# Bias store moved behind the last weight split; routing with halved searches, merged top-k lists, host-turned p and an early gather

## The reference, cut to what matters

```
h = RMSNorm(x); qA,kA,vA,qB,kB,vB = h @ W_in
A: windowed attention (|q-k| <= 128), sink logit per head,
   bias rel_bias[t5_bucket(k-q)] shared by all tokens, 8 heads
B: dense attention with normalised q/k and axial rotary positions, 8 heads
x += concat(RMSNorm_A(oA), RMSNorm_B(oB)) @ W_out
h = RMSNorm(x); aff = softmax(h @ W_router)              # 16 experts
per set (sample, prompt): gates, idx = top_k(aff.T, cap) # cap 128 of 1024, 64 of 512
x += scatter_add(idx, gates * (silu(h[idx] @ Wg) * (h[idx] @ Wu)) @ Wd)
x += sigmoid(RMSNorm(x) @ W_pg) * (p @ W_pp)             # p: 256 wide
y = RMSNorm(x)
```

## Time and profile before

| | us |
|---|---|
| three runs | 1563.09, 1562.75, 1559.45 (median 1562.75) |
| profiled execution | 1559.1 (span 1557.1) |
| PE busy | 1429.2 (92%) |
| DVE busy | 919.7 (59%) |
| ACT busy | 725.8 (47%) |
| POOL busy | 183.3 (12%) |
| mean granted TensorE clock | 0.957 |

### The profile page before, as it was taken

How to read it: one execution, slowest core, us unless ns; L and a number is a source line. 1 busy time by engine, 2 the same in 40 slices (tenths; PEclk the granted TensorE clock), 3 DMA queues, 4 the chain that set the end, 5 groups by cost and what they waited for, 6 DMA issues and landing times. The chain is left out here.

```text
span 1557.1 us, 21333 instructions
## 1 busy us (share of the span) xinstructions
PE 1429.2 (92%) x7224; PEld 1006.1 (65%) x7224; DVE 919.7 (59%) x1324; ACT 725.8 (47%) x1157; POOL 183.3 (12%) x257
## 2 busy tenths in 40 slices
PE   7979997999999798699999699999999999959997
PEld 6758886656555555478877566666666666628885
DVE  4624443777776588432367847766676676653544
ACT  4534444777766577322223444445444444432332
POOL 1111110000000000000001201211121121021110
PEclk9989997999999889799998899999999999979999
DMA  7464465211222133444433747787788778672331
GB/s 297 117 156 160 148 212 200 77 68 66 85 96 99 52 134 126 158 147 137 162 108 127 273 172 252 253 268 256 257 275 274 254 252 262 237 243 75 128 135 68
DMA packets 83709, 267.28 MB, mean 172 GB/s; under 512 B 7968, under 2 KB 37792, under 8 KB 68296
## 3 DMA queue, kind: packets, MB, share of 16 engines
q1 hardware_dynamic: 75456, 239.32, 42.5%
q0 software_dynamic: 7168, 25.17, 7.0%
q10 hardware_dynamic: 1032, 2.10, 1.2%
HBM read 199.98 MB, written 66.58 MB: 171 GB/s over the span
## 5 line engine op out<-in xcount | busy, mean ns | idle before, releaser
L1875 DVE TENSOR_TENSOR moe_w_lo<-ring,moe_w_hi 128x2048 fp32r<-128x2048 f32 x96 | 220.3, 2296 | 157.4 <-ACT moe_w_hi L1814 157.4
L1814 ACT ACTIVATE moe_w_hi<-ring 128x2048 fp32r<-128x2048 f32 x96 | 183.6, 1914 | 201.2 <-PE moe_p_g L1997 122.8
L1525 PE MATMUL mix_p_big<-kept_out_w,mix_m_hi 128*128 128x512 f32 x384 | 126.9, 412 | 4.6 <-DVE mix_m_lo L1400 2.4
L550 PE MATMUL proj_p_out<-proj_w_hi,proj_h_hi 128*128 128x512 f32 x288 | 118.5, 411 | 10.4 <-DVE proj_w_lo L461 10.3
L2005 PE MATMUL moe_p_gu<-ring,moe_xT_r 128*64 128x512 f32 x512 | 116.9, 598 | 0.0
L550 PE MATMUL proj_p_out<-proj_w_hi,proj_h_lo 128*128 128x512 f32 x288 | 113.9, 395 | 0.0
L550 PE MATMUL proj_p_out<-proj_w_lo,proj_h_hi 128*128 128x512 f32 x288 | 113.7, 395 | 0.0
L1073 DVE TENSOR_REDUCE sample_ntop<-sample_p_s 128x1 f32<-128x1024 f32 x64 | 78.1, 1222 | 41.7 <-PE sample_p_s L896 40.9
L910 PEld LDWEIGHTS sample_p_t<-kept_ident_r,sample_probs_r 128*128 128x128 f32 x688 | 72.7, 141 | 23.7 <-ACT sample_probs L1011 6.5
L1525 PEld LDWEIGHTS mix_p_big<-kept_out_w,mix_m_hi 128*128 128x128 f32 x384 | 73.0, 195 | 21.5 <-issue 2.7
L910 PE MATMUL sample_p_t<-kept_ident_r,sample_probs_r 128*128 128x128 f32 x688 | 80.0, 246 | 4.9 <-ACT sample_probs L1011 2.4
(11 more groups left out here) (292 smaller groups left out, 3059.6 us busy)
## 6 DMA issues: line engine op xcount, KB each, us to landing
ring<-in_w_gate SPq DMA_DIRECT2D x32, 1024.0 KB, 5.1
ring<-in_w_up SPq DMA_DIRECT2D x32, 1024.0 KB, 7.0
ring<-in_w_down SPq DMA_DIRECT2D x32, 1024.0 KB, 5.7
qT_d<-proj_qT SPq DMA_DIRECT2D x12, 1024.0 KB, 3.8
proj_xT<-in_xT SPq DMA_DIRECT2D x12, 512.0 KB, 3.9
proj_w_raw<-in_w_in SPq DMA_DIRECT2D x8, 768.0 KB, 6.6
proj_x<-in_x SPq DMA_DIRECT2D x12, 512.0 KB, 5.7
kT_d<-proj_kT SPq DMA_DIRECT2D x12, 512.0 KB, 3.5
```

The lines of the kernel that those rows point to most:

```text
L550: mm = pe.matmul(p_out[:, s, cols], h[:, s, k, :], w[:, k, cols], start=(k == 0 and n == 0), stop=(k == KC - 1 and n == 2))
L1525: mm = pe.matmul(p_out[:, cols], m[:, s, k, :], ww[:, k, cols], start=(k == 0 and n == 0), stop=(k == KC - 1 and n == 2))
L1814: act.activation(w_hi[:, at % SPLIT], raw[:, at % RAW], ACT.Copy).then_inc(hi_made, 1)
L1875: dve.tensor_tensor(w_lo[:, at % SPLIT], raw[:, at % RAW], w_hi[:, at % SPLIT].bitcast(F32), ALU.subtract).then_inc(lo_made, 1)
```

## The change

**Bias rows.** They are loaded between weight chunks 2 and 3. PE looks them up after chunk 3 of `first_products`, DVE adds before `low_w(5)`, ScalarE stores right behind `high_w(7)`, before the squares of tiles 0 and 1.

```diff
@@ project_inputs
+            bias.load(sp, rel_bias, hot, outside)      # SP, after load_w(2)
             load_w(3)
...
                 high_w(k)
+            bias.store(act, rel_d)
             square(0, 0)
...
+                if k == 5:
+                    bias.add(dve)
                 low_w(k)
...
+                    if k == 3:
+                        bias.look_up(pe)
...
-                if isinstance(t, int) and t == 1 and begin == 0:
+                if first and begin == 0:
                     pe.wait_ge(bias.added, 1)
...
             product(2, 0, 0, spread(0))
-            bias.look_up(pe, qk_copied, 6)
```

```diff
@@ mix_and_route
+        SEARCHES = ((0, EXPERTS, S_HALF, CAP), (32, EXPERTS, S_HALF, CAP), (64, 32 + EXPERTS, P_HALF, HALF))
+        ROUNDS = [size // 8 for _, _, _, size in SEARCHES]
+        OPS = [3 * n - 1 for n in ROUNDS]
...
+            def step(t, s, takes):
+                searches = 1 if t < SAMPLE_TILES + 2 else 2
                 if inside(t):
                     low(t, s)
                 if inside(t - 3):
-                    copy_aff(t - 3, 1 - s)
-                search(first, last)
+                    copy_aff(t - 3)
+                searching.take(takes[0], searches)
                 if inside(t - 1):
                     add_x(t - 1, 1 - s)
                 if inside(t - 2):
                     top(t - 2)
+                searching.take(takes[1], searches)
                 if inside(t - 1):
                     norm(t - 1, 1 - s)
                 if inside(t - 2):
                     affinity(t - 2)
+                searching.take(takes[2], searches)
...
+            for t in range(1, N):
+                step(t, t % 2, (6, 2, 6) if t >= SAMPLE_TILES // 2 + 2 else (0, 0, 0))
+            copy_aff(N - 3)
+            searching.take(6)
+            add_x(N - 1, 1)
+            top(N - 2)
+            searching.take(1)
+            affinity(N - 2)
+            norm(N - 1, 1)
+            copy_aff(N - 2)
+            searching.take(8)
             top(N - 1)
+            searching.take(1)
             affinity(N - 1)
-            copy_aff(N - 1, 1)
...
+            searching.take(sum(OPS))
+            list_sample()
+            copy_aff(N - 1)
+            search(2, 0, 6)
+            merge(0, 0, S_HALF, 0)
+            search(2, 6, OPS[2])
+            list_prompt()
+            merge(1, PROMPT_ROW, P_HALF, T_SAMPLE)
```

**p.** The host gives p transposed; one load brings all of it. ScalarE rounds it (`split_p`, one operation), POOL makes the low part, both now with four buffers (AHEAD = 4) instead of two, as has the product `ple`. `product_p(0)` goes to the PSUM area of the turned input and no longer waits for `add_x`; `product_p(1)` waits for it. PE's order at the end:

```diff
             turn_m(0, 0)
             run(pe, step, N)
-            turn_p(0, 0)
-            turn_p(1, 1)
             step(N, 0)
...
+            product_p(0)
+            product_p(1)
             turn_aff(N - 2)
             turn_h(N - 1, 1)
...
+            product_p(2)
             logits(N - 1)
...
+            product_p(3)
             turn_aff(N - 1)
...
+            product_p(4)
+            turn_lists(0)
+            for t in range(5, 8):
+                product_p(t)
+            turn_lists(1)
+            for t in range(8, N):
+                product_p(t)
```

**Gather.** POOL gathers expert 0's rows in the routing stage, behind its last `low_p`:

```diff
+            for t in range(AHEAD, N):
+                low_p(t)
+            for s in range(2):
+                pool.wait_ge(h_stored[s], 8 * N)
+            pool.wait_ge(mm_done, 2 * N)
+            pool.wait_ge(handed, 2)
+            expert_rows.gather_sample(pool, 0)
+            pool.wait_ge(handed, 4)
+            expert_rows.gather_prompt(pool, 0)
```

In `experts` the split of the first turned rows goes ahead of the second weight unit's on ACT and DVE, the first `gate_up` waits for two of the three parts, and PE turns the prompt rows of expert 0 behind its first unit instead of ahead of it:

```diff
             split(0, 0)
+            x_high(0)                                  # DVE: x_low(0)
             split(0, 1)
-            x_high(0)
...
-                    pe.wait_ge(t_out, x_round(e) + X_ROUNDS)
+                    pe.wait_ge(t_out, x_round(e) + X_ROUNDS - 1)
...
+                    if is_int(e) and e == 0 and j == 0:
+                        turn_x_prompt(0)
```

More of the change, by code:

```diff
@@ L1378, in _ @@
                 w_p.high(act, k)
[L1379 to L1388, removed]
+            for t in range(1, 4):
+                step(t, t % 2)
+            for t in range(AHEAD):
+                split_p(t)
             with act.Fori(2, N // 2) as i:
                 for k in range(2):
[L1391 to L1394, removed]
+                    step(i * 2 + k, k)
+            step(N, 0)
+            out_p(0)
+            copy_hT(N - 1)
+            out_p(1)
+            softmax(N - 1)
+            for t in range(2, N):
+                out_p(t)
         @block.vector
@@ L1427, in affinity, with copy_aff @@
                 dve.tensor_scalar(aff[:], e_r[:], share[:], None, ALU.mult).then_inc(aff_made, 1)
[L1429 removed]
+            def copy_aff(t):
                 dve.wait_ge(affT_made, t + 1)
[L1431 to L1436 removed]
@@ L1438, in search @@
-            def search(first, last):
+                if t < SAMPLE_TILES:
+                    row, c = 32 * (t // 4), t % 4 * P
+                else:
+                    row, c = 32 * (2 + (t - SAMPLE_TILES) // 2), t % 2 * P
+                dve.tensor_copy(work[row:row + EXPERTS, 0, c:c + P], p_aff).then_inc(affT_out, 1)
+            def search(which, first, last):
+                row, n_rows, tokens, _ = SEARCHES[which]
+                rows = slice(row, row + n_rows)
+                rounds_ago, strikes_ago = sum(ROUNDS[:which]), sum(n - 1 for n in ROUNDS[:which])
@@ L1458, in search, with backwards, list_sample @@
                         dve.match_replace(there, best[rows, eight], here, -1.0).then_inc(struck, 1)
-            def step(t, s, first=0, last=0):
+            def backwards(ap):
+                step, n = ap.ap[1]
+                return bass.AP(ap.tensor, ap.offset + (n - 1) * step, [ap.ap[0], [-step, n]])
+            def list_sample():
+                dve.wait_ge(indexed, sum(ROUNDS[:2]))
+                one, two = slice(0, EXPERTS), slice(32, 32 + EXPERTS)
+                dve.tensor_copy(place[one, :], at[one, :]).then_inc(listed, 1)
+                dve.tensor_copy(value[one, :], best[one, :]).then_inc(listed, 1)
+                dve.tensor_copy(place[two, :], backwards(at[two, :])).then_inc(listed, 1)
+                dve.tensor_copy(value[two, :], backwards(best[two, :])).then_inc(listed, 1)
@@ new lines, in list_prompt @@
+            def list_prompt():
+                dve.wait_ge(indexed, sum(ROUNDS))
+                for row, order in ((64, lambda ap: ap), (96, backwards)):
+                    rows = slice(row, row + EXPERTS)
+                    for out, ap in ((place, at), (value, best)):
+                        dve.tensor_copy(out[rows, :].rearrange("p (a c) -> p a c", a=2),
+                                        order(ap[rows, 0:HALF]).unsqueeze(1).broadcast_to([EXPERTS, 2, HALF])).then_inc(
+                                            listed, 1)
@@ new lines, in _, with __init__, take @@
+            class Searching:
+                def __init__(self):
+                    self.which, self.done = 0, 0
+                def take(self, n, searches=2):
+                    while n and self.which < searches:
+                        part = min(n, OPS[self.which] - self.done)
+                        search(self.which, self.done, self.done + part)
+                        self.done, n = self.done + part, n - part
+                        if self.done == OPS[self.which]:
+                            self.which, self.done = self.which + 1, 0
@@ L1744, in _ @@
             step(E)
-            for s in range(2):
-                sp.wait_ge(ple_stored[s], 8 * TILES)
+            for done in ple_stored:
+                sp.wait_ge(done, 16 * TILES // len(ple_stored))
             for m in range(PG_UNITS):
@@ L1777, in scatter @@
                         compute_op=ALU.add).then_inc(added, 16)
-            for e in range(3):
+            for e in range(1, 3):
                 gather(e)
```

236 lines of the change are left out of this document (115 added, 121 removed).

## The result

The changed kernel takes 1553.33 us (median of 9 runs, 1548.97 to 1556.5), the kernel before on the same chip 1559.91 us (9 runs, 1556.94 to 1564.61). The ratio is 0.9947, with a 95% interval of 0.9932 to 0.9962: 6 to 11 us faster, where 26 were forecast. 1553.33 lies just above the range's upper end of 1553. The profiled execution took 1551.5 us with a span of 1549.5, so its span is 7.6 us shorter than before's 1557.1.

A forecast was written before the change was run, and what follows sets the result against it. TensorE, busy 92% of the span, was taken as the bound, so only its losses could be won. Bias part 12 plus routing part 14 made 26 us: 1533 for the profiled execution, 1537 on the median's scale, range 1525 to 1553.

The forecast's parts named there:

- Bias part, removed: Projection: moving the bias store removes TensorE's 11.2 us idle at 80 us and 2.1 us of clock, 13.5 us at most.
- The cover for lookup and add: Projection: lookup after chunk 3 and add before split 5 cost nothing; if the cover failed, 3 us.
- Bias part, added: Projection: tile 0's qT_d store, behind the moved bias store, lands in 12.5 us, 1.5 us late; bias part nets +12.
- rival 3: Projection: the bias store does to tile 0 what it did to tile 1, 26.9 us; 1553 us in all; chance 12%.
- Search operations: Routing, VectorE: a top-8 operation shrinks with its width, from 1.25 us to 0.72 at 512 and 0.45 at 256.
- rival 2: Routing: narrow top-8 operations cost as much as wide ones; 1606 us, slower; chance 7%.
- Steps and the first ple product: Routing loop: six steps lengthen by 0.4 us each, yet the first ple product starts at 828.4, 7.9 us earlier.
- Rival 1: Routing: the clock falls in the six lengthened steps, some 2.2 us a place; gain 15, 1548 us; chance 20%.
- Ple products: Routing: twelve products of 2.73 us; TensorE stands 4.3 us for the prompt lists and ends at 869.
- End of the stage: Routing: after ScalarE's copy and SP's store and weight load, the stage ends about 870.5 against 880.16, 9.7 us earlier.
- Experts' start: Experts: 11.5 us from slots to first expert matmul become 5.9; the prompt rows' turn between the first units costs 0.6.
- The sum: Whole kernel: bias part 12 plus routing part 14 gives 26 us, 1533 for the profiled execution.

The follow-up runs named there:

- run 3: Changed kernel with the bias rows held twice, stored from 16 partitions instead of 8, 64 rows each: 1536.85 us, ratio 0.9836 to the kernel before.
- run 1: Kernel before with the bias part of the change alone: 1561.46 us, ratio 1.0001 to the kernel before.
- run 2: Changed kernel with the bias part undone, so the routing part alone: 1553.43 us, ratio 0.9942 to the kernel before.
- run 8: Changed kernel with bias store on 16 partitions, prompt lists turned behind ple product 9, first prompt gather issued in the experts stage: 1528.93 us, ratio 0.9791.
- Run 6: Changed kernel with TensorE's turn of the prompt lists behind ple product 9 instead of 7: 1548.68 us, ratio 0.9917 to the kernel before.
- run 7: Changed kernel with bias store on 16 partitions and prompt lists turned behind ple product 9: 1532.44 us, ratio 0.9813 to the kernel before.

## Why the prediction was wrong

**Bias part, removed: right.** The stall was worth about the 13.5 us that the prediction gave it: run 3, which has it nowhere, ends the projection 13.2 us before the changed kernel and 14.2 before the kernel before. The cover for lookup and add held: no new wait of TensorE stands near 25 us.

**Bias part, added: the step that failed.** "At 49.6 the bias store is 23 us old, not 8, and its early backlog has been worked off: I take 12.5 us". There is no early backlog that is worked off. The store is quick only in its first 3 us (34 rows a us), then moves 24 a us until 64 us and 13 in the last 10 us, which it shares with SP's queue. It lasts from 28 to 74 us, and at 50 us it was as much in the way as ever. qT_d landed after 21.2 us: 10.8 us of stand and some 3 of clock (0.50 from 70.9 to 78.2 us) instead of 1.5. The range of the term was right (-4 to +13.5) and run 1 put it at 0; the value was taken at the wrong end, against the only row with a store of qT_d inside a bias store. My rival 3 was the mechanism, at 12%.

I had also dismissed that row's meaning. I took the q's store as "eight rows an engine" that would each wait for one bias row. The trace of the changed kernel fits longer turns: nothing on q1 in 57 to 63 us, while each of the 8 busy engines passed 144/8 = 18 bias rows, and nothing in 39 to 50 us, 264/8 = 33 rows, with a store open on q1 both times. The Trainium skill ("DMA: Bandwidth & Descriptors", Queues, rings and completion order) says an engine changes queues only after a whole packet, which is several descriptors long; I had read a packet as one row. The trace agrees that an engine stays for many rows; but where the page gives 9 to 17 descriptors as typical and 64 as the most, 33 rows and more passed here before SP's queue had its turn. Why the store uses 8 engines is told by the same page (Why a DMA increments its semaphore by 16 and not by 1): the number of engines is the largest up to 16 that divides the outermost dimension of both sides, here 8 heads. Run 3 agrees, with 16: q10's share went from 47% to 76% and, in 34 to 40 us, 83%.

**Search operations: right,** 0.72 and 0.46 us; rival 2 is out. MAX8 at 512 takes 674 to 685 ns in all 32 instances, FIND_INDEX8 672 to 686 and MATCH_REPLACE8 662 to 676, so POOL's work beside them did not stretch them.

**Steps and the first ple product: 7.9 forecast, 5.4 measured** from the first W_out product on. Of the missing 2.4 us, 0.8 are there at product 9 already: the first 14.4 us of W_out products ran at clock 0.79 and not 0.88 as before, 1.3 us, while steps 6 to 8 lengthened by some 0.8 us, less than the 1.2 forecast. The other 1.6 is the clock at 815 us, at half behind 0.92 us of idle (1.7 us). Rival 1 was therefore right in kind and not in count. Such a fall came once in the changed kernel, twice in run 2, and not at all in run 8, whose idle before the same product was the same 0.9 us. One profiled execution does not tell how many there will be.

**Ple products: the second step that failed.** The stand was forecast at 4.3 us and measured at 4.54. What the prediction left out is what a stand does to the matmuls behind it: thirteen at half speed, 2.6 us, though it had priced just this for the stall at 80 us. Run 6 measures 7.3 us for both. In all the products took 44.1 us where 40.6 were forecast (828.4 to 869).

**End of the stage: 1.3 us more.** From the end of the last product to ScalarE's first split it is 2.8 us, not 1.5. **Experts' start: right.** The first expert matmul comes 5.5 us after that split starts (5.9 forecast). Prompt turn and slow matmuls then take 1.3 us, not 0.6.

**The sum.** Of 26 us forecast for the profiled execution 7.6 came: the bias part gave about 0 for 12, the routing part about 7 for 14. For routing: 2.4 late at the first product, 3.5 in the products, 1.3 at the stage's end, less 0.4, is 6.8 us: 15.3 forecast for the first expert matmul less 8.5 measured.

## What to carry to other kernels

A transfer that slows its neighbours has a duration and an engine count; before moving it, lay its whole drain over every deadline of the new place, and if it covers one there, change its shape instead: here the move was worth nothing, and the same bytes from twice as many partitions, on twice as many engines, 16 us. Where a row shows the very collision, take its number and not an argument that it should be milder. And price an idle stretch of TensorE with the slow matmuls behind it, up to 3 us here, wherever it lies.

## What the hardware showed

- A store of the same 1024 rows of 2 KB moved 24 rows a us from 8 source partitions (0.32 us a row on 8 engines), 49 from 16 (0.27 on 16 engines) and 94 from 128 (0.088 on 16 engines). The first 100 rows from 8 partitions (28 to 31 us of the changed kernel) took only 0.085 us each. A step of 20480 bytes between copies in place of 20484 changed nothing. Whether the number of source partitions, their number an engine or the larger steps do it is open.
- A slow store on ScalarE's queue holds SP's as well: SP's issues took up to 7.7 us in the changed kernel, and 0.35 us in run 3 at the same places.
- The end of the routing stage waited for GpSimd's gather under way (2.9 us in run 7). How the wait comes about isn't shown.
- How often the clock falls behind less than 1 us of idle varied from none to two in the same code; why is open.
